# Spare TensorE products in every pause of a router stage, on one core of a Trainium2 chip

## What is computed

```python
hf = rmsnorm(x, g_ffn)
lg = hf @ w_rg + b_rg                      # 4 groups
g_sel = argmax(lg)
le = (hf @ w_re + b_re)[group g_sel]       # 8 experts of that group
top_p, top_i = top_k(softmax(le), 2)       # two experts for each row
for e in range(32):
    gu = hf @ w_e_in[e]
    act = silu(gu[:, :256]) * gu[:, 256:]
    out += gates[:, e] * (act @ w_e_out[e])
x = x + out
```

## Time and profile before

| | us |
|---|---|
| runs of the kernel, median of 3 | 614.89 (614.53, 614.89, 617.66) |
| the profiled execution, its own time | 614.02 |
| its span, first to last instruction | 612.3 |
| TensorE busy in the span | 547.3 (89%) |
| VectorE, ScalarE, GpSimd busy | 283.7, 162.2, 119.6 |
| chain that ended last: TensorE, DMA, VectorE | 68%, 12%, 7% |

### The profile page before, as it was taken

The page is one execution under the profiler, slowest core; times in us unless marked ns, Lnnn a source line. Parts: engine busy times, 40 slices in busy tenths (PEclk is TensorE's granted clock), DMA queues, the critical chain, the costliest instruction groups (busy, mean ns, idle before and its releaser), DMA issues.

```text
span 612.3 us, 7898 instructions
## 1 busy us (share of the span) xinstructions
PE 547.3 (89%) x3041; PEld 322.7 (53%) x3042; DVE 283.7 (46%) x489; ACT 162.2 (26%) x259; POOL 119.6 (20%) x184
## 2 busy tenths in 40 slices
PE   3999999999999898799999799999997879789893
PEld 2448999999765544344554664434332323233340
DVE  2532799999776646474365851111211101011246
ACT  3122122321766775662110200101010001000122
POOL 3131000302352341501001231111220201201002
PEclk9999999999999999999999699999998979889998
DMA  8801745400600600059842489999999999999994
GB/s 289 212 1 48 262 157 187 139 1 1 213 2 14 262 1 0 1 158 380 314 163 81 150 306 425 422 423 423 426 425 423 427 422 425 426 418 422 404 321 152
DMA packets 43899, 148.90 MB, mean 243 GB/s; under 512 B 7029, under 2 KB 23437, under 8 KB 35160
## 3 DMA queue, kind: packets, MB, share of 16 engines
q1 hardware_dynamic: 39399, 139.63, 58.7%
q0 software_dynamic: 4464, 8.80, 3.8%
HBM read 136.29 MB, written 19.59 MB: 255 GB/s over the span
## 4 chain that ended last, share of the span: by engine, by line
PE 68%; DMA 12%; DVE 7%; SPq 5%; ACT 4%; issue 2%; POOL 0%; DVEq 0%; ACTq 0%
PE ps L959 17%; PE ps L1361 12%; DMA big<-in_w_expert_in 11%; PE ps L1184 8%; PE ps L1386 5%; PE ps L930 5%; SPq L616 3%; PE ps L1442 3%; PE ps L1069 2%; SPq L566 2%; PE ps L1028 2%; PE ps L1345 1%; PE ps L1066 1%; PE ps L1090 1%; DVE big L1840 1%
## 5 line engine op out<-in xcount | busy, mean ns | idle before, releaser
L1361 PE MATMUL ps<-big,cw 128*64 128x512 f32 x352 | 84.2, 632 | 13.1 <-issue 6.7
L1765 DVE SCALAR_TENSOR_TENSOR big<-low,cwt,big 128x590 f32<-128x590 f32 x120 | 95.2, 855 | 0.4
L2139 DVE TENSOR_TENSOR low<-low,ps 128x256 f32<-128x256 f32 x16 | 6.7, 421 | 180.6 <-ACT low L1644 180.6
L959 PE MATMUL ps<-cw_r 128*128 128x288 f32 x256 | 73.0, 295 | 0.0
L959 PE MATMUL ps<-low_r,cw_r 128*128 128x288 f32 x256 | 72.8, 294 | 0.0
L959 PE MATMUL ps<-cw_r,big_r 128*128 128x288 f32 x256 | 72.7, 294 | 0.0
L1361 PEld LDWEIGHTS ps<-big,cw 128*64 128x64 f32 x352 | 29.7, 145 | 65.7 <-issue 65.5
L1184 PE MATMUL ps<-cw,low 128*128 128x512 f32 x128 | 56.7, 594 | 0.2 <-DVE low L1884 0.2
L959 PEld LDWEIGHTS ps<-cw_r 128*128 128x128 f32 x256 | 47.4, 188 | 0.4 <-issue 0.4
L1386 PE MATMUL ps<-big,low 128*64 128x512 f32 x176 | 40.2, 597 | 7.9 <-DVE low L2145 7.9
L959 PEld LDWEIGHTS ps<-cw_r,big_r 128*128 128x128 f32 x256 | 47.2, 188 | 0.0
(11 more groups left out here) (271 smaller groups left out, 783.0 us busy)
## 6 DMA issues: line engine op xcount, KB each, us to landing
big<-in_w_expert_in SPq DMA_DIRECT2D x20, 2048.0 KB, 24.8
big<-in_w_expert_out SPq DMA_DIRECT2D x22, 1024.0 KB, 29.7
low<-in_w_expert_in SPq DMA_DIRECT2D x8, 2048.0 KB, 25.8
big<-in_w_in SPq DMA_DIRECT2D x20, 512.0 KB, 5.2
low<-in_w_expert_out SPq DMA_DIRECT2D x10, 1024.0 KB, 31.0
y_dram<-big SPq DMA_DIRECT2D x9, 512.0 KB, 5.2
cw<-in_w_out SPq DMA_DIRECT2D x1, 4096.0 KB, 14.2
low<-in_w_expert_in SPq DMA_DIRECT2D x4, 1024.0 KB, 36.1
```

Source lines behind the costliest of these rows:

```text
L959: return pe.matmul(ps[:, proj_bank(j) + half, 0:HALF], w[:, k, :], h[:, k, cols], start=first, stop=last, skip_group_check=True)
L1361: mm = pe.matmul(ps[TILE * half:TILE * half + TILE, GU_BANK[s], :], xt[s][:, k, TILE * half:TILE * half + TILE], wi[2 * s + half][:, k, :] ...
L1765: ins = dve.scalar_tensor_tensor(conv[:, i, :], u[:, i, j:j + CW], cwt[:, i, j:j + 1], conv[:, i, :], ALU.mult, ALU.add)
```

## The change

Four more groups of spare products are issued, and one is made longer: 18 in place of 6 ahead of chunk 3's logits, then 4 ahead of chunk 4's transposes, 6 ahead of chunk 4's logits, 12 ahead of the last positions, and 4 ahead of the tables of chunks 2 to 4. The 12 behind the totals stay. Nothing else is touched.

```diff
             positions(2)
             pe.wait_ge(x2_ready, 4)
+            busy(18)
+            logits(3)
+            busy(4)
+            turn_h2(4)
             busy(6)
-            logits(3)
-            turn_h2(4)
             logits(4)
             positions(3)
             for c in range(2):
                 table(c)
+            busy(12)
             positions(4)
+            busy(4)
             for c in range(2, NC):
                 table(c)
             totals()
```

## The result

| | before | after |
|---|---|---|
| median of 16 runs each, us | 614.96 (614.00 to 617.69) | 619.09 (616.63 to 622.33) |
| ratio of the times, 95% interval | | 1.0058 (1.0040 to 1.0076) |
| profiled execution, own time / span, us | 614.02 / 612.3 | 621.41 / 619.7 |
| granted clock, mean | 0.971 | 0.969 |

The change makes the kernel slower by 0.6%, some 3.6 us. The forecast was 616.5 with a range of 614.3 to 619.2, so the time lies just inside its upper end. Three single executions further down, one each of the kernel before, e6_fit and e9_idle, took 818 to 1120 us in a slow state and are left out of every ratio.

The account below looks back on a forecast made before the run. The expert weight stream, started by the first gather behind a chain of small router steps, was taken to bound the kernel: 2.9 us of products less 1.15 of faster steps gave +1.8, forecast 616.5 us, range 614.3 to 619.2.

Parts of the forecast that it names:

- Steps 1 to 3: Chunk 3's logits 1.8 us later, chunk 4's transposes start 2.4 later, take 0.75 at full clock, end 2.05 later.
- Step 5: Chunk 4's logits take 1.1 us at full clock in place of 1.90, so VectorE's choice starts 1.75 later.
- The rule from the Trainium skill: A weight load takes its columns divided by 1.2, in ns, whatever the clock; transposes gain nothing, sum +2.15, 616.9 us.
- the scaling: Chunk 4's narrow transposes and logits get faster with the clock: 0.35 + 0.8 = 1.15 us given back.
- Step 4: 6 products behind chunk 4's transposes take 1.4 us; its logits start 0.4 past the pause they fill.
- step 7: 4 products ahead of the last tables end level with VectorE's last places, 351.05; tables done 1.8 us later.
- Step 6: 12 products make the last positions 2.4 us later, covered by VectorE's slack of 0.8 us.
- Step 8: The gather takes 4.96 us from table reading to first turn, at 357.1; TensorE waits 2 us for it.
- Step 9: Behind the gather all keeps its length, 1.8 us later; the weight stream has no reserve at its two gates.
- The first rival: Clock holds up to the gather and falls there, slowing pair 0's gate_up; up to +3.5 us, 618.2; 16%.
- The rival of products at half clock: Clock in the router stage not held, so spare products run at half clock; +6.3 us, 621.0; 13%.
- a possible gain: In the no-change rival (10%, 614.7 us): slow runs of before may pay up to 1.7 us the new kernel never pays.

Follow-up runs that it names:

- e6_fit: Changed kernel with groups cut to the pauses, 9, 0, 3, 7, 4 products, and 20 behind the totals; 619.11 us, ratio 1.0032 to the kernel before.
- e9_idle: Changed kernel with none in place of 12 products behind the totals; 619.62 us, ratio 1.0049 to the kernel before.
- e8_notab: e3_fill without the 4 products ahead of the last tables; 617.60 us, ratio 1.0047 to the kernel before.
- e3_fill: Changed kernel with 20 in place of 12 products behind the totals; 618.27 us, ratio 1.0059 to the kernel before.
- e7_over: e3_fill with 30 in place of 20 products behind the totals; 620.32 us, ratio 1.0070 to the kernel before.
- e10_again: The changed kernel measured and profiled once more without an edit; 619.31 us, ratio 1.0042 to the kernel before.
- e2_rest: Changed kernel with 6 in place of 18 products ahead of chunk 3's logits; 619.00 us, ratio 1.0058 to the kernel before.

## Why the prediction was right or wrong

**Steps 1 to 3** held to a few hundredths: 18 products put chunk 3's logits 1.79 us later (1.8), the transposes 2.43 (2.4), and at full clock these took 0.71 us (0.75). **Step 5** held in its size, logits 1.12 us where I had 1.1.

**The rule from the Trainium skill** on weight loads ("TensorE: Matmul & The Clock Gate", "LDWEIGHTS (loading the stationary operand)") fell: by it the transposes could not get faster, and they went from 1.11 to 0.71 us with the clock. Keeping the scaling was right.

**Step 4** was 0.2 us short: its twelve records start 0.1 later behind the transposes and take 1.54 us to the next step (347.92 to 349.46), where 0.08 + 12 x 0.111 gives 1.4. Each group costs that bit more, 24 records from first to next step 2.87 and not 2.75.

**Steps 6 and 7 are where the sum failed**, by 0.8 us in all with what step 4 left short. From the transposes of chunk 4 to the tables TensorE now runs without a wait, so its small shortfalls add up: the last positions came 2.94 later, not 2.4, and the last tables started 15.25 us behind the mark, where step 7 had 14.49 (351.05). Step 6 was right that VectorE's slack covers the late positions: its last places came 2.03 later (1.75). But TensorE's own row has no such slack. In step 7 I compared the end of the four products with VectorE's last places and found them level, and missed that two of three tables behind the products need not wait for those places at all. They have to be done before the last table, so products and two tables must fit ahead of it, and they don't. Without the products, in e8_notab, the tables are done at 15.54 and the first turn is at 20.56, both 1.83 later than before, which is the forecast's 1.8; e3_fill less e8_notab gives the products as 0.85 us. The sum to the gather was +1.8, measured +2.63.

**Step 8** held: 5.02 us from reading the table to the turn (4.96), and a new wait of 1.88 (2). **Step 9** was half right. What is late at the first gate is late at the end: the last column of the table of experiments stays within 0.7 us over eight executions and over 6.6 us of shift of the first turn. But the second gate has a reserve of about 2 us; e7_over shows 1.9 of it.

**The first rival**, given 16%, came in both profiles of the changed kernel: the clock holds up to the gather and falls there. Its price was set at up to 1.7 us on the second gate and passed on in full; the gate lost 3.1 us (turn and gate table are slower as well), the reserve took 2 and the end lost about 1. Its sign was named beforehand, a clock of 0.5 anywhere in 341 to 362; it shows in the 0.75 of 360 to 365. From the mark to the end the changed kernel took 3.6 us longer than the kernel before in its first profile, 3.8 in its second, and e3_fill, whose clock held there, 2.7. So 2.6 us of path and 1 of the fall make 3.6, which is the measured 0.58%. That the ratio is just that is partly chance, since how often the clock falls there was not measured.

**The rival of products at half clock** did not come in a profile of the changed kernel. e6_fit shows its mechanism with fewer products.

**The chances.** The direction and most of the mechanism were right, but the sum had half of the loss, 1.8 of 3.6 us. That 619.09 still lies inside the range is owed to the room left for this rival and the next, not to the sum. Within 0.5% had 74% and slower 23%; measured is 0.58% with an interval from 0.40 to 0.76, on the slower side of the border. And I had put the spread of the runs of before into a remark, as a possible gain; it is the same in both kernels, and no gain came from it.

## What to carry to other kernels

Work that is to fill a pause must end before the pause does, and must be counted against the whole row of steps up to the next fixed point, not against the one step next to it: 4 products ahead of three tables looked hidden and cost 0.85 us. Holding TensorE's clock is worth only what the clocked steps have on the path, and here most of the path is VectorE's and the gather's (0 and 6 products ahead of the steps gave the same time, 44 gave 0.6% more). Before judging small changes by a median, look into the traces for a mark ahead of the change: here the clock's fall in an untouched stage moves everything by up to 4 us.

## What the runs showed of the hardware

- The clock of TensorE in one and the same code differs between executions. The mark ahead of the change lay at 336.5 to 336.7 (three executions), 337.7 to 338.5 (four) and 340.2 to 340.6 (five), with no, one or two, and three falls in the attention stage. At the first gather, behind the same last steps and a wait of 1.9 us, it fell in two executions (after, e10_again) and held in one (e2_rest).
- Once fallen, the clock did not come back by the small steps of the router stage, only behind or within a dense stretch (before, in the 24 records from 350.56 on, after some 4 us of them); in e6_fit, whose TensorE was busy throughout from 345 to 355, it stayed at half for those ten microseconds though no wait was left in them.
- Narrow float32 steps were faster at full clock, with few columns of weights or many. Chunk 4's eight transposes (128 columns of weights, 64 streamed) took 1.11 us at half clock and 0.71 at full; its logits (64 columns of weights, 36 streamed) took 1.90 and 1.12 for 16 records, with the last record taken off 0.107 and 0.059 us each.
